# The last attention of a four-layer fp32 kernel: another order for its output projection, and two weight tiles whose low parts GpSimd makes

## The reference, cut to what matters

```python
s = einsum('bqhd,bkhd->bhqk', qb, kb) * scale + bias   # block-causal
p = softmax(s)
attn = p[:, :, 0] - lam_full * p[:, :, 1]
o = einsum('bhqk,bkhe->bqhe', attn, vb)
o = o * rsqrt(mean(o * o) + SUBLN_EPS) * subln_g * (1 - lambda_init)
y = o @ w_o
x = layer_norm(alpha * x + y);  x = layer_norm(alpha * x + square(relu(x @ w1)) @ w2)
```

## Time and profile before

| | us |
|---|---|
| median of 3 runs | 1306.3 |
| lowest and highest run | 1305.62 and 1308.9 |
| the profiled execution's own time | 1305.0 |
| span of that execution, first to last instruction | 1303.2 |

### The profile page before, as it was taken

How to read it: one execution, slowest core, us unless ns; L and a number is a source line. 1 busy time by engine, 2 the same in 40 slices (tenths; PEclk the granted TensorE clock), 3 DMA queues, 4 the chain that set the end, 5 groups by cost and what they waited for, 6 DMA issues and landing times.

```text
span 1303.2 us, 23675 instructions
## 1 busy us (share of the span) xinstructions
PE 1272.9 (98%) x10059; PEld 1101.9 (85%) x10059; DVE 894.3 (69%) x1467; ACT 679.4 (52%) x1228; POOL 84.2 (6%) x103
## 2 busy tenths in 40 slices
PE   8999999999999999999999999999999999999997
PEld 6978888889967888888898997888897987788886
DVE  6886666674585666666998848666668366766676
ACT  6875444463484454544673534444545477445452
POOL 3000500000061000000001600000000000000000
PEclk9999999999999999999999999999999999999999
DMA  9445454444411555543353003555555441455550
GB/s 350 157 185 201 185 191 185 188 181 158 167 66 65 215 193 193 187 188 144 132 193 131 4 26 111 224 194 194 194 194 190 175 161 71 180 194 194 194 194 33
DMA packets 17496, 214.45 MB, mean 165 GB/s; under 512 B 1960, under 2 KB 2128, under 8 KB 4720
## 3 DMA queue, kind: packets, MB, share of 16 engines
q1 hardware_dynamic: 15888, 205.43, 41.8%
q0 software_dynamic: 1504, 7.52, 1.5%
HBM read 211.87 MB, written 1.06 MB: 163 GB/s over the span
## 4 chain that ended last, share of the span: by engine, by line
PE 82%; DVE 9%; ACT 7%; DMA 1%; issue 1%; SPq 0%; DVEq 0%; ACTq 0%
PE psum L696 25%; PE psum L670 14%; PE psum L676 7%; PE psum L486 4%; PE psum L487 4%; PE psum L488 4%; DVE w_low L2000 3%; ACT w_high L1447 2%; PE psum L1058 1%; PE psum L1202 1%; PE psum L585 1%; PE psum L1249 1%; PE psum L581 1%; DMA ring<-weights 1%; PE psum L577 1%; PE psum L1377 1%
## 5 line engine op out<-in xcount | busy, mean ns | idle before, releaser
L2000 DVE TENSOR_TENSOR w_low<-ring,w_high 128x1024 fp32r<-128x1024 f32 x372 | 443.2, 1227 | 193.4 <-ACT w_high L1447 193.4
L1447 ACT ACTIVATE w_high<-ring 128x1024 fp32r<-128x1024 f32 x372 | 372.8, 1048 | 134.0 <-PE psum L696 105.5
L696 PE MATMUL psum<-w_high,up_split 128*128 128x512 f32 x1024 | 287.6, 391 | 0.8 <-DVE up_split L2155 0.8
L696 PEld LDWEIGHTS psum<-w_high,up_split 128*128 128x128 f32 x1024 | 190.3, 188 | 40.5 <-issue 2.7
L670 PE MATMUL psum<-act_split,w_high 128*128 128x512 f32 x768 | 191.6, 391 | 0.0
L696 PE MATMUL psum<-w_low,up_split 128*128 128x512 f32 x512 | 163.2, 390 | 0.0
L670 PEld LDWEIGHTS psum<-act_split,w_high 128*128 128x128 f32 x768 | 139.6, 189 | 26.0
L1548 ACT ACTIVATE up_split<-work 128x256 fp32r<-128x256 f32 x112 | 46.8, 418 | 159.4 <-DVE work L2148 148.8
L486 PE MATMUL psum<-act_split,w_high 128*128 128x256 f32 x448 | 129.5, 289 | 0.1
L487 PE MATMUL psum<-act_split,w_high 128*128 128x256 f32 x448 | 126.7, 283 | 0.0
L488 PE MATMUL psum<-act_split,w_low 128*128 128x256 f32 x448 | 126.6, 283 | 0.0
(11 more groups left out here) (361 smaller groups left out, 1882.0 us busy)
## 6 DMA issues: line engine op xcount, KB each, us to landing
ring<-weights SPq DMA_DIRECT2D x95, 2048.0 KB, 7.5
work<-rows POOLq DMA_DIRECT2D x4, 1024.0 KB, 5.0
ring<-weights SPq DMA_DIRECT2D x4, 512.0 KB, 8.5
work<-rows POOLq DMA_DIRECT2D x4, 512.0 KB, 5.4
x<-x_in SPq DMA_DIRECT2D x2, 512.0 KB, 4.6
work<-t_bias POOLq DMA_DIRECT2D x1, 1024.0 KB, 8.1
out<-x SPq DMA_DIRECT2D x4, 256.0 KB, 2.1
con<-consts SPq DMA_DIRECT2D x1, 576.0 KB, 21.5
```

The lines of the kernel that those rows point to most:

```text
L696: last = mm(bank(acc[(th, n)]), up_split[:, m, a, P * th:P * th + P], w[:, f], start=start and i == 0, stop=stop and i == len(pairs) - 1, ...
L1447: A(high[:, HIGH_SLOT[name], f], ring[:, n % RING, f], ACT.Copy).then_inc(weights_high, 1)
L2000: V.tensor_tensor(low[:, n % RING, f], ring[:, n % RING, f], high[:, HIGH_SLOT[name], f].bitcast(f32), ALU.subtract).then_inc(weights_spli ...
```

## The change

- At norms 6 and 7 POOL makes the four low quarters of `da_v0` and `up3_0` (`pool_split`); DVE makes none of these. ACT's high quarters of `up3_0` are spread: the first before the root, two between root and turned copies, the last behind these.
- The first two turns of results move into the last projection (steps 59 and 61); turns and values of head 2 come four steps earlier. Output chunks stand between a head's turns and its values.
- The end goes by token halves: first all that th 0 needs of both column halves, then th 1. At norm 7 DVE thus adds both column halves of th 0 first. Accumulator banks follow.
- ACT and DVE make the last three quarters of `da_o1` behind head 7 and not within the heads.

```diff
-SPLIT_AT, HIGH_SLOT, PAIR_BEFORE = {}, {}, {}
+POOL_TILES = ["da_v0", "up3_0"]
+SPLIT_AT, LOW_AT, HIGH_SLOT, PAIR_BEFORE = {}, {}, {}, {}
+        LOW_AT[_name] = _n - 4 * sum(_t in _order for _t in POOL_TILES)
...
-_mixer_turns(3)
+_norm_turns(7, [(0, 0), (0, 1), (1, 0), (1, 1)], banks=(0, 2, 1, 3))
...
-                pe.wait_ge(weights_split, SPLIT_AT[name] + quarter + 1)
+                if name in POOL_TILES:
+                    pe.wait_ge(sig("pool_split"), 4 * POOL_TILES.index(name) + quarter + 1)
+                else:
+                    pe.wait_ge(weights_split, LOW_AT[name] + quarter + 1)
...
                     da_scores(step // 16)
-                if step in (25, 41, 57):
+                if step in (25, 41, 53):
                     da_transposes(step // 16 - 1)
-                if step in (29, 45, 61):
+                if step in (29, 45, 57):
                     da_values(step // 16 - 1)
-
-            def out_chunk(k, n=0):
+                if step in (59, 61):
+                    out_transposes((step - 59) // 2)
+
+            def out_chunk(k, n=0, ths=(0, 1)):
                 w_hi, w_lo = split_tile(f"da_o{n}")
                 quarter_in(f"da_o{n}", k // 2)
                 read_out(pe, TURN[("dot", k)])
                 f = slice(k * 512, k * 512 + 512)
-                for th in range(2):
+                for th in ths:
                     q = ACC[7][(th, n)]
...
+            da_transposes(3)
             da_scores(4)
-            out_transposes(0)
-            out_transposes(1)
-            da_transposes(3)
+            out_chunk(0)
             da_values(3)
             da_scores(5)
             out_transposes(2)
-            out_chunk(0)
+            out_chunk(1)
             da_transposes(4)
             out_transposes(3)
+            out_chunk(2)
             da_values(4)
-            out_chunk(1)
             da_scores(6)
-            out_chunk(2)
+            out_chunk(3)
             da_transposes(5)
             out_transposes(4)
             da_values(5)
-            out_chunk(3)
             da_scores(7)
             out_chunk(4)
             da_transposes(6)
             out_transposes(5)
+            out_chunk(0, 1)
             da_values(6)
             out_chunk(5)
-
-            out_chunk(0, 1)
             da_transposes(7)
             out_transposes(6)
+            out_chunk(1, 1)
             da_values(7)
-            out_chunk(1, 1)
             out_chunk(6)
+            out_chunk(2, 1, (0,))
+            out_chunk(3, 1, (0,))
             out_transposes(7)
-            out_chunk(2, 1)
-            out_chunk(7)
-            project_out("da_o", 7, act_split, halves=(1,), ks=range(3, NC))
+            out_chunk(4, 1, (0,))
+            out_chunk(5, 1, (0,))
+            out_chunk(7, 0, (0,))
+            out_chunk(6, 1, (0,))
+            out_chunk(7, 1, (0,))
+            out_chunk(7, 0, (1,))
+            for k in range(2, NC):
+                if k == NC - 1:
+                    norm(7, 0)
+                out_chunk(k, 1, (1,))
             mlp(3, 2)
...
                         square(i, *half)
-                if next_tile:
+                if i == 7:
+                    split(next_tile, [0])
+                elif next_tile:
                     split(next_tile)
                 if i < 5 and order[2] == (0, 1):
                     square(i, 0, 1)
                 root(i, 0)
                 if i < 5 and order[2] == (1, 0):
                     square(i, 1, 0)
+                if i == 7:
+                    split(next_tile, [1, 2])
                 out(0)
+                if i == 7:
+                    split(next_tile, [3])
                 if i < 5:
...
             probs(3)
+            head_normed(2)
+            filled(TURN[("da_k", 3)])
+            out_high(0)
             feature_major("da_k", DA_K, 3)
-            head_normed(2)
+            turned(3)
+            out_high(1)
             split("da_o1", [0])
-            turned(3)
-            out_high(0)
-            out_high(1)
             probs(4)
+            out_high(2)
             head_normed(3)
-            out_high(2)
             turned(4)
             out_high(3)
             probs(5)
             head_normed(4)
-            split("da_o1", [1])
             turned(5)
             out_high(4)
             probs(6)
             head_normed(5)
-            split("da_o1", [2])
             turned(6)
             out_high(5)
             probs(7)
             head_normed(6)
             turned(7)
             out_high(6)
+            split("da_o1", [1])
             head_normed(7)
+            split("da_o1", [2])
+            out_high(7)
             split("da_o1", [3])
-            out_high(7)
             norm(7, "up3_0")
...
                 add_in(i, *order[0])
-                if i % 2:
+                if order[1] == (1, 0):
                     add_in(i, *order[1])
-                quarter(0)
+                if i != 7:
+                    quarter(0)
                 if i == 5:
...
                 apply(i, 0)
-                if i in (6, 7):
+                if i == 6:
                     quarter(1)
                 if order[2] == (1, 0):
                     add_in(i, 1, 0)
+                if i == 7:
+                    quarter(0)
                 if i != 7:
                     quarter(2)
                 if i not in (4, 8):
                     acts_low(i, 0, 0)
                     acts_low(i, 0, 1)
+                if i == 7:
+                    quarter(1)
                 add_in(i, 1, 1)
...
             mlp(2, None)
-            norm(6, "da_v0")
+            norm(6)
...
             head_mix(3)
+            out_low(0)
             head_logits(4)
+            out_low(1)
             split("da_o1", [0])
-            out_low(0)
-            out_low(1)
             head_mix(4)
+            out_low(2)
             head_logits(5)
-            out_low(2)
             out_low(3)
             head_mix(5)
             head_logits(6)
-            split("da_o1", [1])
             out_low(4)
             head_mix(6)
             head_logits(7)
-            split("da_o1", [2])
             out_low(5)
             head_mix(7)
             out_low(6)
+            split("da_o1", [1, 2])
             out_low(7)
             split("da_o1", [3])
-            norm(7, "up3_0")
+            norm(7)
             mlp(3, None)
...
             pool.dma_start(da_bias, src).then_inc(sig("bias_in"), 16)
+            def split(name):
+
+                n = TILE_AT[name]
+                for quarter in range(4):
+                    pool.wait_ge(weights_high, SPLIT_AT[name] + quarter + 1)
+                    f = slice(1024 * quarter, 1024 * quarter + 1024)
+                    G.tensor_tensor(low[:, n % RING, f], ring[:, n % RING, f],
+                                    high[:, HIGH_SLOT[name], f].bitcast(f32), ALU.subtract).then_inc(sig("pool_split"), 1)
+
+            split("da_v0")
             next_rows(7)
+            split("up3_0")
             next_rows(8)
```

More of the change, by code:

```diff
@@ L99, with _norm_turns @@
 ACC, TR = {}, {}
-def _norm_turns(i, order, transposes=True):
+def _norm_turns(i, order, transposes=True, banks=range(4)):
     ACC[i], TR[i] = {}, {}
@@ L108, in _norm_turns @@
                 TR[i][(0, n)] = len(BANK) - 1
-        _turns(("acc", i, half), 1, j)
+        _turns(("acc", i, half), 1, banks[j])
         ACC[i][half] = len(BANK) - 1
@@ L187 @@
                (("da_q", 3), 1), (("dscore", 2), 2), (("dpT", 1), 1), (("dpv", 1), 1), (("da_k", 2), 1),
-               (("dscore", 3), 2), (("dpT", 2), 1), (("dpv", 2), 1), (("da_k", 3), 1)]:
+               (("dscore", 3), 2), (("dpT", 2), 1), (("dpv", 2), 1)]:
     _turns(_n, _w)
-for _k, _u in [("dscore", 4), ("dot", 0), ("dot", 1), ("dpT", 3), ("dpv", 3),
-               ("dscore", 5), ("dot", 2), ("dpT", 4), ("dot", 3), ("dpv", 4),
+_turns(("dot", 0), 1, BANK[TURN[("dscore", 3)] + 1])
+_turns(("dot", 1), 1)
+_turns(("da_k", 3), 1, (BANK[TURN[("dpv", 2)]] + 1) % 8)
+for _k, _u in [("dpT", 3), ("dscore", 4), ("dpv", 3), ("dscore", 5), ("dot", 2), ("dpT", 4), ("dot", 3), ("dpv", 4),
                ("dscore", 6), ("dpT", 5), ("dot", 4), ("dpv", 5), ("dscore", 7), ("dpT", 6), ("dot", 5), ("dpv", 6),
```

## The result

The changed kernel takes 1311.8 us (median of 13 runs, 1308.9 to 1316.4) against 1306.05 for the kernel before (13 runs, 1305.2 to 1311.1); the ratio is 1.0042, with a 95% interval of 1.003 to 1.0055. It is slower by 5.7 us. The forecast was 1307.5 and no change that can be measured; the time lies just above the range given. The rival "POOL slower than its small operations show" had said 1311.

What follows compares the result with a forecast made beforehand. PE, busy 98% of the span, bounds the kernel, so only its waits can be gained. Attention -1.5, norm 6 +0.6 and +0.6, norm 7 +1.7 give +1.4 on 1305.0; with 1.3 for the median, forecast 1307.5 us, range 1298 to 1311.5.

Steps and rivals of the forecast that it cites:

- POOL slower than its small operations show: Rival, chance 0.18: the quarter writes fp32r and takes 2.45 us, with 0.7 more of half clock; 1311 us.
- The mechanism: Norms 6 and 7: DVE lines 2032 and 2046, reading two SBUF operands, wait until a POOL operation under way ends.
- 0.8 for th 1 at norm 7: PE's wait for token half 1 at norm 7, 0.8 us, counted among that norm's losses of 7.0.
- 0.5 for the bank of logits 7: Attention: a new PE wait of 0.5 us ahead of chunk 0 of n = 1.
- What a POOL quarter costs: Both norms: a 128 x 1024 low quarter on POOL takes 2.1 us, estimated between 1.90 and 2.2.
- the prediction's own rule: Both norms: a POOL quarter 0.1 us longer or shorter moves the total by 0.8 us.
- the half clock: Slow PE clock behind long waits: costs 1 us at norm 6, 0.6 entering the sum; 0.5 at norm 7.
- norm 6: Norm 6: plus 0.6 us for th 1's late turns and plus 0.6 for slow clock.
- attention: Attention: PE's waits fall from 5.7 to 4.2 us, minus 1.5; bounds minus 3 and plus 0.5.
- norm 7: Norm 7: POOL's first three quarters delay DVE; PE's losses go from 5.3 to 7.0 us, plus 1.7.
- the first rival: Rival, chance 0.20: lines 2032 and 2046 don't wait for POOL; minus 8.5 us, 1297.8.
- The gain as drawn: Rival, chance 0.20: without DVE waiting, norm 6 gains 2.3 us, norm 7 4.7, attention 1.5; 1297.8.

Runs made afterwards that it cites:

- experiment 3: Changed kernel with each POOL quarter issued as four operations of 128x256 instead of one of 128x1024; 1307.05 us, ratio 1.0009 to the kernel before.
- experiment 10: Changed kernel plus 16 POOL multiplications of 128x512 behind norm 8, varying the operands; 1.09 us with second operand from constants, 1.26 from working buffers; no median given.
- 9: Changed kernel plus 12 POOL operations behind norm 8, all else idle; 1.26 us at 128x512, 2.34 at 128x1024; no median given.
- experiment 7: Changed kernel plus 30 POOL subtractions behind norm 7, f32 or fp32r; shortest 128x512 took 1.29 and 1.33 us; no median given.
- Experiment 5: Changed kernel with six quarters on POOL, four of them behind DVE's `normed` signal for th 0, `up3_0`'s last two on DVE; 1300.1 us, ratio 0.9962 to before.
- 4: Changed kernel with only `da_v0`'s first two low quarters on POOL, the other low quarters on DVE; 1304.1 us, ratio 0.9990 to the kernel before.
- 8: Changed kernel plus 40 POOL operations of 128x512 behind norm 7, subtractions and multiplications, full or repeated operand; shortest 1.29 to 1.35 us; no median given.
- experiment 1: Changed kernel with all eight low quarters back on DVE, new order kept; 1305.1 us, ratio 0.9998 to the kernel before.
- 2: Changed kernel with only `da_v0`'s four low quarters on POOL, `up3_0`'s back on DVE; 1308.0 us, ratio 1.0023 to the kernel before.

## Why the prediction was wrong

**The mechanism was right.** Lines 2032 and 2046 (now 2054 and 2068) wait for a POOL operation as line 2000 does; no other engine became the bound, and most waits stand at the places named: 4.10 ahead of norm 6's first turn (forecast some 3), 4.17 and 1.67 at norm 7 (3.6 and 2.1), 1.2 for `da_o1` (1.2). Two that were forecast did not appear: 0.8 for th 1 at norm 7 and 0.5 for the bank of logits 7. The page SBUF — State Buffer of the Trainium skill, section SBUF: two separate sides, describes such waiting as a lock that the first to start holds for the whole instruction. The traces agree, 2.62 to 2.88 us for single operations of 0.75, and experiment 3 shows the "whole instruction" by cutting it.

**What failed are two terms of the sum, both too small.** The first is "What a POOL quarter costs". The term 2.1 us measured 2.37 to 2.40 where no one disturbs it. Its reason was wrong in a way that can be named: the row of 128x512 was taken because its operands "have as many elements as the quarter's". One of them was a mask of 64 columns from the constants, and with both operands from working buffers the same form takes 1.26 (experiment 10). By the prediction's own rule, 0.8 us for 0.1 a quarter, 0.28 more is 2.2 us. That alone would give 1309.7, inside the range.

The page GPSIMD Engine Reference of the Trainium skill, section 4.1 Engine selection, has POOL about twice as slow as DVE with two inputs. The trace agrees: 2.38 against 1.22 is 1.95. The prediction set this rule behind rows of another form.

**The second term is the half clock.** At norm 6 it was priced at 1 us, of which 0.6 entered the sum; it cost 1.5 by the timelines above, and no wait for th 1 was left for it to hide in. At norm 7 the term was 0.5, and it cost 3.3 in the profiled execution, 2.1 and 1.9 in experiments 9 and 10.

| terms, us | forecast | measured | difference |
|---|---|---|---|
| norm 6 | +1.2 | +2.7 | 1.5 |
| attention | -1.5 | -1.1 | 0.4 |
| norm 7 | +1.7 | +4.1 | 2.4 |
| sum | +1.4 | +5.7 | 4.3 |

At norm 6 four quarters of 0.28 more make 1.1 of the difference, and the clock took 0.9 more than its part in the sum; the 0.5 that this is too much is a remainder that was not followed up. The prediction also has a slip here: from 981.5, three quarters of 2.1 end at 987.8 and not at 987.6. At norm 7 the longer quarter is the smaller part: DVE's four operations took 8.94 us where the prediction's own numbers, 2.96 and three times 1.8, give 8.4. The waits of PE came to 5.8 us in all, less than the 6.5 forecast, since none fell on th 1; the clock took 2.8 more than its term, and 0.3 stays without a place. No experiment here sets how long the clock stays low: at the same waits this differs from one execution to the next (last section).

**The attention** lacks 0.4 us of its forecast gain. Of its new waits 0.5 at head norm 3, 0.5 for mix 6 and 1.2 for `da_o1` were expected; 0.8 for mix 7 was not.

**The rival "POOL slower"** had 0.18, and its 1311 came nearest. Some of that is luck: its quarter of 2.45 is longer than the 2.38 measured, its clock of 0.7 more is too short, and its reason, that the quarter writes fp32r, fell in experiment 7.

**A remark on the first rival.** "The gain as drawn" held that without the waiting the attention and norm 7 would gain 1.5 and 4.7 us. No run here is that kernel. Experiment 5 gained 2.9 there, but in it two quarters of `up3_0` stand on DVE and a wait of 1.75 us for th 1 is left.

## What to carry to other kernels

In all runs here, work handed to GpSimd took time from VectorE whenever it met a VectorE operation with two SBUF inputs; place it beside operations that read PSUM or a single operand (4 and 5: 1.15 and 2.1 us gained at norm 6), let it wait for a signal of VectorE if need be, or cut it so that a collision costs one small piece (3). Take the price of such an operation from a row whose operands lie where the new ones will lie, not only from one of the same shape. Where a forecast lets PE wait for some us, give the slow clock behind the wait a range of its own: behind waits of 3.5 to 4.2 us it cost between nothing and 3.3 us here. And when a stretch of the path gets longer although the engine lost work, look for operations in it that are longer than the same line elsewhere.

## What the runs showed of the hardware that was not expected

- GpSimd's multiplication of 128x512 takes 1.09 us with its second operand in the constants and 1.26 with it in a working buffer, all else idle (10); a subtraction in working buffers takes 1.26 too (9). Beside the other engines the figures are 1.09 and 1.29 to 1.35 (7 and 8).
- The same wait of 3.51 us at the same turn of norm 7 was followed by a granted clock of 1.00 in experiment 1 and of 0.50 in experiments 4 and 2. From `da_k0` to `down3_1` these three kernels have the same code and the same waits up to that turn; they differ by 0.5 us (-1.15 and -0.65) and by 1.6 (-1.15 and +0.41). Views by stretches of experiments 1, 4 and 2:

```profile
1117.00:1121.00 4.00, 3.33 (x18) 2.69 (x19) 3.96 (x5) 2.61 (x5) 0.53 (x1) 1.00 0.18 78
```

```profile
1116.00:1119.00 3.00, 3.00 (x10) 2.40 (x9) 3.00 (x3) 1.20 (x3) 0.53 (x1) 0.50 0.55 175
```

```profile
1120.00:1126.00 6.00, 5.50 (x17) 4.63 (x18) 5.96 (x8) 3.10 (x5) 0.53 (x1) 0.50 0.48 175
```

So the length of a wait alone tells neither whether the clock falls behind it nor for how long.
